# Two more norms of a two-block transformer layer by token halves

## The reference

```python
def first_block(x, mem, ...):
    h = x
    h = _layer_norm(ALPHA * h + 0.5 * _swiglu(h, ffn1...), ln1_g, ln1_b)          # norm 1
    h = _layer_norm(ALPHA * h + _token_mixers(h, ...), ln2_g, ln2_b)              # norm 2
    xa = _memory_cross_attention(h, mem, ...)                                     # ends with o @ wo
    h = _layer_norm(ALPHA * h + xa, ln3_g, ln3_b)                                 # norm 3
    h = _layer_norm(ALPHA * h + 0.5 * _swiglu(h, ffn2...), ln4_g, ln4_b)          # norm 4
    return h

def modulate(x, cond, norm_g, w_ada, b_ada):                                      # starts the second block
    shift, scale, gate = jnp.split(jax.nn.silu(cond) @ w_ada + b_ada, 3, axis=-1)
    return rms_norm(x, norm_g) * (1 + scale) + shift, gate                        # the modulated norm
# then z = modulated @ w_in: neighbourhood attention, two convolution branches, merge
```

## Time and profile before

| what | us |
|---|---|
| median of 3 runs (1751.47 to 1753.6) | 1752.1 |
| the profiled execution, its own time | 1754.92 |
| its span (first to last instruction) | 1753.3 |
| TensorE busy | 1719.0 (98%) |
| DVE, ACT, POOL busy | 983.3, 681.0, 149.0 |
| mean granted TensorE clock | 0.995 of full |
| load of one weight strip, issue to landing, median | 3.5 |

### The profile page before, as it was taken

One profiled execution on the slowest core, in us unless ns is written; L12 is line 12 of the kernel. 1 busy time (PEld: TensorE's weight loads), 2 busy tenths in 40 slices (PEclk: granted clock), 3 DMA queues, 4 the chain that ended last, 5 costly groups with the idle time before them and its releaser, 6 DMA issues.

```text
span 1753.3 us, 22917 instructions
## 1 busy us (share of the span) xinstructions
PE 1719.0 (98%) x8534; PEld 1409.0 (80%) x8534; DVE 983.3 (56%) x1323; ACT 681.0 (39%) x961; POOL 149.0 (8%) x154
## 2 busy tenths in 40 slices
PE   8999999999999999999999999999999999999999
PEld 7888888788787788886888888876777777788887
DVE  4333339977964674457333333447967769744442
ACT  4222231245445465534222222235444545732221
POOL 0000000012004611012000000003011020000000
PEclk9999999999999999999999999999999999999999
DMA  5332347633221344223333333332332322143331
GB/s 198 96 97 95 99 140 235 221 97 116 73 73 53 128 135 154 61 73 96 101 97 98 98 96 100 96 105 67 92 98 70 96 83 81 61 132 108 108 99 70
DMA packets 50757, 183.87 MB, mean 105 GB/s; under 512 B 5696, under 2 KB 5952, under 8 KB 50304
## 3 DMA queue, kind: packets, MB, share of 16 engines
q1 hardware_dynamic: 44640, 161.50, 29.4%
q10 hardware_dynamic: 5040, 16.00, 2.8%
q0 software_dynamic: 1008, 5.41, 0.9%
HBM read 180.79 MB, written 2.10 MB: 104 GB/s over the span
## 4 chain that ended last, share of the span: by engine, by line
PE 84%; DVE 9%; ACT 2%; DMA 2%; issue 2%; POOL 0%; SPq 0%; ACTq 0%; DVEq 0%
PE proj L372 76%; DVE w_lo L364 2%; DVE ada_prod L1030 1%; DVE y L1851 1%; ACT w_hi L357 1%; PE aux L1696 1%; DMA ctxv<-ada_in 1%; DVE h L645 1%; PE aux L1683 1%; PE aux L1488 1%; PE proj L1509 1%; DMA ctxk<-ada_in 1%; PE aux L1673 1%; DMA h<-x_in 0%; DVE score L1123 0%
## 5 line engine op out<-in xcount | busy, mean ns | idle before, releaser
L364 DVE TENSOR_TENSOR w_lo<-raw,w_hi 128x1024 fp32r<-128x1024 f32 x303 | 383.0, 1265 | 418.4 <-ACT w_hi L357 411.5
L372 PE MATMUL proj<-a_hi,w_hi 128*128 128x512 f32 (+1 forms) x1536 | 603.0, 393 | 9.7 <-DVE a_lo L651 4.4
L372 PE MATMUL proj<-a_hi,w_lo 128*128 128x512 f32 (+1 forms) x1536 | 592.9, 386 | 0.0
L372 PE MATMUL proj<-a_lo,w_hi 128*128 128x512 f32 (+1 forms) x1536 | 592.6, 386 | 0.0
L357 ACT ACTIVATE w_hi<-raw 128x1024 fp32r<-128x1024 f32 x303 | 318.6, 1053 | 233.8 <-PE proj L372 170.8
L372 PEld LDWEIGHTS proj<-a_hi,w_hi 128*128 128x128 f32 x1536 | 289.6, 189 | 76.3 <-DVE a_lo L651 6.6
L372 PEld LDWEIGHTS proj<-a_lo,w_hi 128*128 128x128 f32 x1536 | 290.0, 189 | 58.9 <-issue 2.9
L372 PEld LDWEIGHTS proj<-a_hi,w_lo 128*128 128x128 f32 x1536 | 289.5, 189 | 58.6
L372 PE MATMUL proj<-hid_hi,w_hi 128*128 128x512 f32 (+1 forms) x374 | 142.2, 380 | 0.0
L372 PE MATMUL proj<-hid_hi,w_lo 128*128 128x512 f32 (+1 forms) x374 | 140.8, 377 | 0.0
L372 PE MATMUL proj<-hid_lo,w_hi 128*128 128x512 f32 (+1 forms) x374 | 140.8, 377 | 0.0
(11 more groups left out here) (342 smaller groups left out, 1999.5 us busy)
## 6 DMA issues: line engine op xcount, KB each, us to landing
raw<-stream SPq DMA_DIRECT2D x303, 512.0 KB, 3.5
ctxk<-ada_in ACTq DMA_DIRECT2D x12, 512.0 KB, 3.9
ctxv<-ada_in ACTq DMA_DIRECT2D x12, 512.0 KB, 4.2
out<-h ACTq DMA_DIRECT2D x8, 256.0 KB, 2.0
h<-x_in SPq DMA_DIRECT2D x3, 512.0 KB, 7.6
btab<-rpb_in POOLq DMA_DIRECT2D x4, 384.0 KB, 3.5
cond_row<-cond_in ACTq DMA_DIRECT2D x1, 1024.0 KB, 6.1
side<-mem_in POOLq DMA_DIRECT2D x1, 1024.0 KB, 5.2
```

The source lines that it names most:

```text
L364: nc.vector.tensor_tensor(w_lo[:, st.slot], raw[:, st.slot], w_hi[:, st.slot].bitcast(F32), ALU.subtract).then_inc(lo_ready, 1)
L372: mm = nc.tensor.matmul(dst, a, b, start=start and n == 0, stop=stop and n == 2)
```

## The change

Norms 3, 4 and the modulated norm become halved: `HALVED = [0, 4, 5, 6]` (the counters of semaphores follow). Around norm 3 the last `wo` strip goes by halves, with four opening sums ahead of its second half, and the first four strips of FFN 2 go staggered. Around norm 4 the last down strips go as in norm 1; the modulated norm of half 0 runs between the parts of norm 4; its statistics for half 1 are matmuls inside the staggered first pass of the neighbourhood part. The idle matmuls go. Splits ahead of the first four strips are issued one strip further ahead. Cut to its core:

```diff
-        HALVED = [0]
+        HALVED = [0, 4, 5, 6]
@@ pe_ffn, first four strips
-                    strip_two_pairs(pe, Nth(s0), Nth(g0), ready)
+                    strips_staggered(pe, Nth(s0), Nth(g0), 0, (0, 0, 1, 3), half_ready_of(pe, ready, 0))
+                    strips_staggered(pe, Nth(s0), Nth(g0), 1, (0, 1, 3, 5), half_ready_of(pe, ready, 1))
@@ pe_na, first four strips
-                    strip_two_pairs(pe, st, g, lo_ready_of(pe, MODN))
+                    beside = {n: lambda c=n - 2: pe_mod_stats(pe, 1, c, c + 1) for n in range(2, KD)}
+                    strips_staggered(pe, st, g, 0, (0, 0, 0, 0), half_ready_of(pe, MODN, 0), beside)
+                    pe_mod_stats(pe, 1, KD - 2, KD)
+                    strips_staggered(pe, st, g, 1, (0, 1, 3, 5), half_ready_of(pe, MODN, 1))
@@ act_na (and dve_na with split_lo)
-                if not first or j:
-                    split_hi(act, st.plus(3))
+                if not first or j != RING:
+                    split_hi(act, st.plus(RING if first and j < RING else 3))
@@ new helpers (act_mod_squares, pe_mod_stats, act_mod_std, dve_ln4, dve_mod, act_mod_hi), two of them
+        def act_mod_squares(act, b, lo, hi):
+            for c in range(lo, hi):
+                act.wait_ge(n_xn, LN4.c0 + KD * b + c + 1)
+                if c >= 2:
+                    act.wait_ge(n_stat, MODN.t0 + KD * b + c - 1)
+                nc.scalar.activation(sq[:, c % 2, tokens(b)], h[:, c, tokens(b)], ACT.Square,
+                                     bias=LN4.shift(c)).then_inc(n_sq, 1)
+        def dve_ln4(dve, b, lo, hi):
+            if lo == 0:
+                dve.wait_ge(n_std, LN4.s0 + b + 1)
+            for c in range(lo, hi):
...
@@ TensorE around norm 3
-            pe_moments(pe, LN3, beside=lambda: pe_ctxv(pe, 0, 1))
-            pe_ctxv(pe, 1, 4)
+            pe_half_strip(pe, last, LN3.groups[KD - 1], 0, a_hi, a_lo, 0, KD, KD)
+            pe_half_strip(pe, last, LN3.groups[KD], 1, a_hi, a_lo, 0, KD, KD,
+                          {0: lambda: pe_half_open(pe, LN3), 3: lambda: pe_half_mean(pe, LN3, 0),
+                           5: lambda: pe_half_square(pe, LN3, 0)})
+            pe_ctxv(pe, 0, 1)
+            pe_half_mean(pe, LN3, 1)
+            pe_ctxv(pe, 1, 2)
+            pe_half_square(pe, LN3, 1)
+            pe_ctxv(pe, 2, 4)
@@ TensorE around norm 4
-            pe_down(pe, S_DOWN2, G_DOWN2, KF, LN4)
-            pe_moments(pe, LN4)
-            pe_keep_clock(12)
-            pe_stats(pe, MODN)
-            pe_keep_clock(16)
+            pe_down_halves(pe, S_DOWN2, G_DOWN2, KF, LN4)
+            pe_mod_stats(pe, 0, 0, 2)
+            pe_half_mean(pe, LN4, 1)
+            pe_half_square(pe, LN4, 1)
+            pe_mod_stats(pe, 0, 2, KD)
@@ DVE around norm 3
+            dve_half_residual(dve, LN3, 0, last, 1.0 / ALPHA)
+            split_lo(dve, Nth(S_CTXV + 2))
+            dve_half_variance(dve, LN3, 0)
+            dve_half_normalise(dve, LN3, 0, 0, 2)
+            dve_half_residual(dve, LN3, 1, last, 1.0 / ALPHA)
+            split_lo(dve, Nth(S_CTXV + 3))
+            dve_half_normalise(dve, LN3, 0, 2, 3)
+            split_lo(dve, Nth(S_FFN2))
+            dve_half_normalise(dve, LN3, 0, 3, 5)
+            split_lo(dve, Nth(S_FFN2 + 1))
+            dve_half_normalise(dve, LN3, 0, 5, 6)
+            dve_half_variance(dve, LN3, 1)
+            dve_half_normalise(dve, LN3, 0, 6, 7)
+            split_lo(dve, Nth(S_FFN2 + 2))
+            dve_half_normalise(dve, LN3, 0, 7, KD + 1)
+            dve_half_normalise(dve, LN3, 1, 0, 2)
+            split_lo(dve, Nth(S_FFN2 + 3))
+            dve_half_normalise(dve, LN3, 1, 2, KD + 1)
@@ ACT around norm 4
+            act_half_std(act, LN4, 0, chain)
+            act_mod_squares(act, 0, 0, 2)
+            split_hi(act, Nth(S_NA + 2))
+            act_half_square(act, LN4, 1)
+            act_mod_squares(act, 0, 2, 3)
+            split_hi(act, Nth(S_NA + 3))
+            act_mod_squares(act, 0, 3, 4)
+            act_half_mean_square(act, LN4, 1)
+            act_mod_squares(act, 0, 4, KD)
+            act_half_std(act, LN4, 1, chain)
+            act_mod_std(act, 0, chain)
+            for c in range(KD):
+                act_mod_hi(act, 0, c, c + 1)
+                act_mod_squares(act, 1, c, c + 1)
+            act_mod_std(act, 1, chain)
+            act_mod_hi(act, 1, 0, KD)
@@ DVE around norm 4
+            dve_half_variance(dve, LN4, 0)
+            dve_ln4(dve, 0, 0, 2)
+            split_lo(dve, Nth(S_NA + 2))
+            dve_ln4(dve, 0, 2, 3)
+            dve_half_residual(dve, LN4, 1, last, 0.5 / ALPHA)
+            dve_ln4(dve, 0, 3, 4)
+            split_lo(dve, Nth(S_NA + 3))
+            dve_ln4(dve, 0, 4, KD)
+            dve_half_variance(dve, LN4, 1)
+            for c in range(KD):
+                dve_mod(dve, 0, c, c + 1)
+                dve_ln4(dve, 1, c, c + 1)
+            dve_mod(dve, 0, KD, KD + 1)
+            dve_mod(dve, 1, 0, KD + 1)
```

More of the change, by code:

```diff
@@ L446, in __init__ @@
                 self.s0 = sum(2 if n in HALVED else 1 for n in range(k))
-                self.c0 = 8 * self.s0
+                self.c0 = 8 * sum(2 if n in HALVED else 1 for n in range(k) if n != 6)
                 self.r = r
@@ L658, in act_hi, with pool_half_shift @@
                 nc.scalar.activation(m.hi[:, c], m.dst[:, c], ACT.Identity, bias=m.shift(c)).then_inc(n_hi, 1)
+        def pool_half_shift(pool, m, after):
+            for b in range(2):
+                for c in range(KD):
+                    pool.wait_ge(n_sq, after.q0 + KD * b + c + 1)
+                    nc.gpsimd.tensor_scalar(h[:, c, tokens(b)], h[:, c, tokens(b)], 1.0, m.shift(c), ALU.mult,
+                                            ALU.add).then_inc(n_raw, 1)
         def pool_shift(pool, m):
@@ new lines, in act_mod_std @@
+        def act_mod_std(act, b, chain):
+            act.wait_ge(n_stat, MODN.t0 + KD * (b + 1))
+            inverse_root(chain, rstd[:, tokens(b)], aux[:, 2 * b + 1, :HT], MODN.eps).then_inc(n_std, 1)
+        def dve_ln4(dve, b, lo, hi):
+            if lo == 0:
+                dve.wait_ge(n_std, LN4.s0 + b + 1)
+            for c in range(lo, hi):
+                dve.wait_ge(r_cent, 8 * LN4.u + KD * b + c + 1)
+                nc.vector.scalar_tensor_tensor(h[:, c, tokens(b)], h[:, c, tokens(b)], LN4.gain(c), rstd[:, tokens(b)],
+                                               ALU.mult, ALU.mult).then_inc(n_xn, 1)
+                if c + 2 < KD:
+                    dve_half_recentre(dve, LN4, b, c + 2)
@@ new lines, in dve_mod @@
+        def dve_mod(dve, b, lo, hi):
+            if lo == 0:
+                dve.wait_ge(n_std, MODN.s0 + b + 1)
+            for c in range(lo, hi):
+                if c < KD:
+                    dve.wait_ge(n_raw, LN4.r0 + KD * b + c + 1)
+                    nc.vector.scalar_tensor_tensor(hm[:, c, tokens(b)], h[:, c, tokens(b)], MODN.gain(c),
+                                                   rstd[:, tokens(b)], ALU.mult, ALU.mult).then_inc(mod_xn, 1)
+                if c >= 1:
+                    dve.wait_ge(n_hi, MODN.h0 + KD * b + c)
+                    nc.vector.scalar_tensor_tensor(a_lo[:, c - 1, tokens(b)], hm[:, c - 1, tokens(b)],
+                                                   MODN.shift(c - 1), a_hi[:, c - 1, tokens(b)].bitcast(F32), ALU.add,
+                                                   ALU.subtract).then_inc(n_lo, 1)
@@ L833, in lo_ready_of, with act_mod_hi @@
+        def act_mod_hi(act, b, lo, hi):
+            for c in range(lo, hi):
+                act.wait_ge(mod_xn, KD * b + c + 1)
+                nc.scalar.activation(a_hi[:, c, tokens(b)], hm[:, c, tokens(b)], ACT.Identity,
+                                     bias=MODN.shift(c)).then_inc(n_hi, 1)
         def lo_ready_of(pe, m):
@@ L884, in two @@
                     st, g = Nth(s0 + j, 4, i), Nth(g0 + j, 4, i)
-                    if not (quad and first and j == 0):
+                    if not (quad and first):
                         split_hi(act, st.plus(3))
+                    elif j < 3:
+                        split_hi(act, st.plus(4))
                     if j % 2 == 0:
@@ L904, in two @@
                     st, g = Nth(s0 + j, 4, i), Nth(g0 + j, 4, i)
-                    if not (quad and first and j == 0):
+                    if not (quad and first):
                         split_lo(dve, st.plus(3))
+                    elif j < 3:
+                        split_lo(dve, st.plus(4))
                     if j % 2:
@@ L962, in act_down_halves @@
             split_hi(act, Nth(s0 + LAST + 4))
+        def act_down_halves(act, s0, m, chain, beside=None):
+            act_down_seven(act, s0, m, beside)
             act_half_square(act, m, 0)
@@ L1878, in dve_na @@
                     norm(2 * (j - 7) + 1)
-                if not first or j:
-                    split_lo(dve, st.plus(3))
+                if not first or j != RING:
```

(3 more changed lines are left out.)

101 lines of the change are left out of this document (53 added, 48 removed).

## The result

The changed kernel takes 1771.15 us, median of four runs (1770.71 to 1771.73), against 1752.8 for the kernel before, run beside it: ratio 1.0106, interval 1.0088 to 1.0123. It is slower by 18.4 us; 1770.7 was forecast. The profiled execution took 1770.84, its span 1769.1, 15.8 more than the span before. It was already 3.9 us ahead when it reached norm 3, 2.7 of that within the first 330 us, where the kernel before ran at half clock from 12 to 16 and this one at 1.00; so 19.7 were lost behind.

What follows compares the result with a forecast made beforehand. TensorE, busy 98% of the span, was taken as the bound, so only its waits could be won. Norm 3 +3.3, norm 4 onward +11.7, clock +4.1, less 0.5, gave 18.6 on 1752.1: 1770.7 us, range 1759 to 1778.

Steps and rivals of the forecast that it cites:

- Norm 4 and what stands behind it: From norm 4 to the first turn of block 0: 11.7 us later, 4.7 of it TensorE's own, plus 2.4 for clock.
- DVE's waits for splits: At norm 4 DVE waits twice for ACT, which squares first and only then splits: 1.3 and 1.2 us.
- Wait between the passes: Behind norm 4, the second pass needs half 1's last statistic, root and split: TensorE waits 2.9 us.
- wait ahead of the key statistic: Behind the four strips after norm 4, TensorE waits 3.0 us before statistic L1711.
- The 0.5 for small waits later: Small waits later in the kernel may go, taking 0.5 us off the sum.
- The clock: TensorE falls to half speed near sparse stretches: 2.4 us at norm 4 and 1.7 at norm 3, together 4.1.
- DVE is due: Behind norm 4 DVE was already due at the first turn, so late `glu` makes 4.7 us into 11.7.
- Norm 3: 3.3 and 1.7 forecast: At norm 3 the first four FFN strips end 3.3 us later, plus 1.7 for clock.
- my own two signs of being wrong: Wrong if statistic L1711 comes less than 4 later behind the down projection, or TensorE never waits for `w_lo` behind norm 3.
- the step from DVE's list to the long wait: At norm 3 DVE's work and 3.0 us of waiting put strip 2's split at 815.5, so TensorE waits 3.4.
- The waits: TensorE at norm 3: 1.2 us at the opening sums, 0.3 at context strips, 3.4 and 2.4 at strips 2 and 3.
- rival C: Both norms: DVE's half 1 work hides under TensorE's first pass, splits ready when asked; 3 to 6 us faster, 1747; chance 0.07.

Runs made afterwards that it cites:

- E4: Changed kernel with idle matmuls put into TensorE's waits at norm 4; 1768.76 us, ratio 1.0095.
- E6: E4 with 16 more idle matmuls ahead of the first scores; 1769.61 us, ratio 1.0101.
- E7: Changed kernel with five convolution taps of the first neighbourhood iteration moved to the iteration's end; 1767.11 us, ratio 1.0082.
- E1: Changed kernel with only norm 3 halved, norm 4 and the modulated norm as in the kernel before; 1756.70 us, ratio 1.0024.
- E3: Changed kernel with ACT's copies of the context values out of PSUM moved ahead of half 1's inverse root; 1769.47 us, ratio 1.0100.
- E8: E1 with norm 3's lists mended: opening sums later, strips 2 and 3 later, splits and context copies earlier; 1746.96 us, ratio 0.9968.
- E9: E1 with only the opening sums, mean and square of norm 3 moved later on TensorE; 1754.56 us, ratio 1.0014.
- E12: Changed kernel with E8's lists, E7's taps, idle matmuls, second pass in pairs and half 1's statistics a step earlier; 1754.47 us, ratio 1.0012.
- E10: E8 without its opening sums edit, so only the splits and bank edits on E1; 1751.08 us, ratio 0.9989.

## Why the prediction came out right, and where it was off

The medians lie 18.4 apart where 18.6 was forecast. The order of the terms is right, DVE behind norm 4 first; that they meet the total so closely is in part luck: norm 3's terms were off both ways, norm 4's waits were 0.4 above mine and its clock 0.8 below, and in the profiles the change lost 19.7 in the two stretches and had 3.9 in hand from ahead of them.

**Norm 4 and what stands behind it: 11.7 and 2.4 forecast, 13.7 measured.** To compare times, add 2.1 to mine, by which the mid sum moved. First multiply of norm 4: 1180.1 forecast, 1180.11 measured (but the table load of 1.3 that I named as part of the gain stands behind that multiply's root in the kernel before, at 1181.93, and is no part of it). DVE's waits for splits: 1.3 and 1.2, measured 1.19 and 1.15. Wait between the passes 2.9 (2.59), wait ahead of the key statistic (L1711, now L1783) 3.0 (3.10), first product 1195.2 (1196.30), `glu` 1229.0 (1231.95), turn 1254.9 without clock (1256.89). The slip grows between the first product and `glu`, by 1.9, which is what E4 took off `glu` with the clock held. The first `hm` came 1.4 behind half 1's root, within the 1.0 to 1.5 named. The 0.5 for small waits later did not come: the part behind the first turn is as long as before. Without the clock's share the whole is 12.1 (E6), against 11.7.

**The clock.** The fall came in the first pass, as forecast, and its price at norm 4 was 1.6 (E6) rather than 2.4. What I had not seen is that it is no term of its own: E4 gave the same time back at the next wait, and of some 4.8 lost to half speed in the norm 4 stretch only 1.6 reached its end. The Trainium skill ("TensorE: Matmul & The Clock Gate", Part 1) ties the clock to how busy the array has lately been; from that the prediction had worked out 5 to 10 for three sparse stretches. A fall came in each of the three; their price was 1.6 at norm 4 and, by the windows, 3 at norm 3 beyond what the kernel before lost there already.

**DVE is due.** The step that made 4.7 into 11.7. TensorE's own pass ends 1227.7 - 1218.7 - 2.1 = 6.9 late, the turn 13.7; E7 took 3.2 of the difference back with DVE's list alone. Right.

**Norm 3: 3.3 and 1.7 forecast, 6.0 measured.** The six kernels with this norm 3 (after, E1, E4 to E7) took 356.1 to 358.9, mean 357.8, so 4.8 more than before. The sum is near, but by luck: three terms were off and made up for one another. One of my own two signs of being wrong even came: behind norm 3 TensorE never waited for `w_lo` in the profile after. (The other did not: the statistic L1711, now L1783, came 9.9 us later behind the mid sum, not less than 4.) What failed there is the step from DVE's list to the long wait: the bank held TensorE, and the split only behind it. The three terms:
- I took the end of the four strips before at 836.5, the end of the window in the earlier trace rows. That row counts 91 products of 96; the 96 end at 837.9. So my own schedule stood for +1.9, not +3.3.
- The waits. Forecast 1.2, 0.3, 3.4 and 2.4; measured 1.93, none, 4.52, none. The third was put down to `w_lo` of strip 2. That was there at 814.1; TensorE waited until 815.67 for the PSUM bank, since ACT's copies of the context values stood behind `a_hi` of chunk 7. I had left them out of ACT's list as something that TensorE waits for. E3 showed it; with the bank free, `w_lo` held TensorE for 3.19, near the 3.4. The wait for strip 3 never came, probably since strip 2 was late already and TensorE then ran at half speed; no run isolates that.
- The clock: 1.7 forecast for new falls. In the profile after, 2 us windows behind the mid sum stand at 0.87, 0.50, 0.78 at the opening sums and at 0.50 three times behind 815; with TensorE busy in them that is some 4.7 us lost, before it was 1.7. In E1, E6 and E7 it was 3.2 to 3.3, in E4 1.6. Without what half speed costs, the six kernels take 354.2 to 354.5 and the kernel before 351.2: so halving with these lists cost 3.1 by waits and prices, where my schedule had 1.9, and the clock took the rest.

**What halving itself costs.** E8, with one wait of 0.43 and no fall, has 348.4. Before, less its waits (0.59, 2.11, 1.10, 0.42) and 1.7 of clock, is 347.0; E8 less its wait 348.0. So halves cost 1.0 at norm 3; the rest is order, and the clock behind it. That is where rival C went: its mechanism was sound at norm 3, its condition (splits ahead of the instructions that wait for DVE) was not met by the lists as written. It had not named the opening sums, which are worth 2.3 by themselves (E9). Left open: which part of the 5.9 that stay in E12 is price and which is order. Statistics in line with products, 3.4 by my count, are the likeliest part; this was not measured by itself.

## What to carry to other kernels

Halving a norm paid here only once every instruction of the next stage was followed to its end: on ACT, put the split ahead of the `a_hi` that waits for DVE, and list what still holds the accumulators, not only what feeds TensorE. Before the halves are blamed, take the waits out one at a time (E9, E10): the same halving went from 4 us slower to 6 us faster. A stage whose second statistic can't start until the first is applied (norm 4 here) gives less room: with every list tried it stayed 5.9 us or more behind. By the forecast's account, which no run isolates, TensorE lost in statistics in line and in late first strips what it won at its start.

When a term is hidden under another engine, a saving in front of it shows up as a longer wait behind, and that wait may cost clock in turn. An edit that shows nothing by itself (E4) can be worth something once the next wait is covered too (E6, 1.6 us).
